# A one-core hybrid block (RWKV-7, Mamba-2, short convolution): opposite partition halves for head pairs, logits on two row halves, and the second scan moved behind the solve

## The reference, cut to what matters

```python
p = rmsnorm(x, norm_w) @ w_in
pa, pb, pc, pg = split(p)
def step(s, inp):                       # rwkv7, 16 heads of 64
    r_t, w_t, k_t, v_t, kh_t, b_t = inp
    sa = einsum('bhvk,bhk->bhv', s, kh_t)
    s = s * w_t[:, :, None, :] - sa[..., None] * b_t[:, :, None, :] + v_t[..., None] * k_t[:, :, None, :]
    return s, einsum('bhvk,bhk->bhv', s, r_t)
ob = mamba2_branch(pb)                  # conv of 4 taps, chunked scan (128), norm
oc = short_conv_branch(pc)
merged = sum(sigmoid(gates) * (o @ w_branch), axis=2)
out = rmsnorm(x + merged @ w_out, final_norm_w)
```

## Time and profile before

| what | us |
|---|---|
| median of 3 runs | 1234.29 (1234.07 to 1234.81) |
| the profiled execution: time, span | 1233.7, 1232.0 |
| PE busy | 1186.5 (96%) |
| VectorE busy | 798.4 (65%) |
| ScalarE busy | 578.0 (47%) |
| mean DMA rate | 160 GB/s |

### The profile page before, as it was taken

The page is one execution under the profiler, slowest core; times in us unless marked ns, Lnnn a source line. Parts: engine busy times, 40 slices in busy tenths (PEclk is TensorE's granted clock), DMA queues, the critical chain, the costliest instruction groups (busy, mean ns, idle before and its releaser), DMA issues.

```text
span 1232.0 us, 23862 instructions
## 1 busy us (share of the span) xinstructions
PE 1186.5 (96%) x8598; PEld 1057.4 (86%) x8598; DVE 798.4 (65%) x1229; ACT 578.0 (47%) x836; POOL 68.4 (6%) x93
## 2 busy tenths in 40 slices
PE   6998999999999999999999999999999999999996
PEld 5998899898898998989989978888888888888885
DVE  4786858678488585885876856564555565556553
ACT  5454445354364463544545535544444444434443
POOL 2001001010010010100101102000000000000000
PEclk9999999999999999999999999999999999999998
DMA  5755545544555354445554445566666666567662
GB/s 164 206 154 140 156 123 141 140 118 129 143 141 150 102 154 132 136 124 139 143 149 113 128 140 172 171 198 196 192 199 189 190 189 200 190 189 274 200 191 101
DMA packets 254749, 197.27 MB, mean 160 GB/s; under 512 B 23943, under 2 KB 207472, under 8 KB 254064
## 3 DMA queue, kind: packets, MB, share of 16 engines
q1 hardware_dynamic: 254404, 196.08, 55.1%
q10 hardware_dynamic: 300, 0.58, 0.1%
HBM read 193.71 MB, written 2.11 MB: 159 GB/s over the span
## 4 chain that ended last, share of the span: by engine, by line
PE 81%; DVE 11%; issue 3%; ACT 2%; DMA 1%; DVEq 1%; SPq 0%; POOL 0%; ACTq 0%
PE ps L1129 11%; PE ps L1207 11%; PE ps L1208 11%; PE ps L1209 11%; PE ps L1130 10%; PE ps L1131 10%; DVE lots L879 3%; DVE wlo L716 3%; PE ps L1460 2%; PE ps L1459 2%; PE ps L1461 2%; DVE lots L882 2%; ACT whi L421 1%; PE ps L1122 1%; DVE lots L724 1%
## 5 line engine op out<-in xcount | busy, mean ns | idle before, releaser
L716 DVE TENSOR_TENSOR wlo<-raw,whi 128x1024 fp32r<-128x1024 f32 (+1 forms) x356 | 436.0, 1238 | 278.7 <-ACT whi L421 278.1
L421 ACT ACTIVATE whi<-raw 128x1024 fp32r<-128x1024 f32 (+1 forms) x356 | 370.3, 1053 | 273.4 <-PE ps L1209 183.6
L1129 PE MATMUL ps<-hhi,whi 128*128 128x256 f32 (+1 forms) x1440 | 424.6, 295 | 5.7 <-DVE wlo L716 5.7
L1130 PE MATMUL ps<-hlo,whi 128*128 128x256 f32 (+1 forms) x1440 | 406.8, 282 | 0.0
L1131 PE MATMUL ps<-hhi,wlo 128*128 128x256 f32 (+1 forms) x1440 | 406.4, 282 | 0.0
L1129 PEld LDWEIGHTS ps<-hhi,whi 128*128 128x128 f32 (+1 forms) x1440 | 273.4, 190 | 22.6 <-issue 9.8
L1130 PEld LDWEIGHTS ps<-hlo,whi 128*128 128x128 f32 (+1 forms) x1440 | 274.0, 190 | 1.0
L1131 PEld LDWEIGHTS ps<-hhi,wlo 128*128 128x128 f32 (+1 forms) x1440 | 273.7, 190 | 0.3
L1207 PE MATMUL ps<-whi,hhi 128*128 128x512 f32 x384 | 151.4, 394 | 0.0
L1209 PE MATMUL ps<-whi,hlo 128*128 128x512 f32 x384 | 149.6, 390 | 0.0
L1208 PE MATMUL ps<-wlo,hhi 128*128 128x512 f32 x384 | 149.5, 389 | 0.0
(11 more groups left out here) (267 smaller groups left out, 1185.4 us busy)
## 6 DMA issues: line engine op xcount, KB each, us to landing
raw<-in_w_in SPq DMA_DIRECT2D x548, 256.0 KB, 3.2
raw<-in_w_branch SPq DMA_DIRECT2D x96, 256.0 KB, 3.7
raw<-in_w_out SPq DMA_DIRECT2D x64, 256.0 KB, 3.6
o<-in_x SPq DMA_DIRECT2D x4, 1024.0 KB, 6.9
acb<-acs_rows SPq DMA_DIRECT2D x8, 256.0 KB, 4.0
out_y<-lots SPq DMA_DIRECT2D x3, 512.0 KB, 4.6
lots<-in_final_norm_w SPq DMA_DIRECT2D x1, 1024.0 KB, 10.3
lots<-ad SPq DMA_DIRECT2D x32, 8.0 KB
```

Of the source, the lines that this page charges most:

```text
L421: sc.activation(whi[:, slot, :, 0:width], raw[:, slot, :, 0:width], ACT.Copy).then_inc(hi_done, 1)
L716: tt(wlo[:, slot, :, 0:width], raw[:, slot, :, 0:width], whi[:, slot, :, 0:width].bitcast(F32), ALU.subtract).then_inc(lo_done, 1)
L1129: mm(dst, a, khi, start=first, stop=False)
L1130: mm(dst, a, klo, start=False, stop=False)
```

## The change

- **Halves.** Head 0 keeps its state in partitions 0 to 63 and its identity in 64 to 127, head 1 the other way round. The products for `yz`, `nm` and the state then write opposite column halves for the two heads. The products with the identity (L1351) go; VectorE adds r times the decay to `yz` itself, in two instructions (`z_in`, slot 24). `gcs` and its products (L1331) go; each state row is scaled by VectorE straight from `gg`, in two instructions of 64 partitions instead of one.
- **Logits.** Each uses only its 64 rows, on its own row half, into two PSUM banks (A and C); PE waits for `var_rt` before it, and ScalarE takes the logits at slot 36 instead of 38.
- **Order.** Scores go one slot earlier (3, 5, 7). SyncE issues two `ad` transfers behind each quarter of a strip. The solve goes to slots 9 to 12; conv to 13, `seg` to 15, `xs2` to 18. The transposes of x go to slot 20 and `yb` to slot 22 on PE. Two of the four `tb` transfers are issued by ScalarE. The head norm goes to slot 34 around `kk_floor`, `kk_recip` and `decays` to 35.

```diff
+V_XT = 20
+V_YB = V_P1 + 4
...
-                strip(c + 8, cols, quarters=range(0, 2))
                 for q in range(4):
                     if q % 2 == 0:
+                        strip(c + 8, cols, quarters=range(q // 2, q // 2 + 1))
                         sp.wait_ge(s["ad_ok"], j * 2 + q // 2 + 1)
                     sp.dma_start(sol_n[8 * q:8 * q + 8, :, :], ad[:, q, :]).then_inc(s["n_in"], 16)
...
                 sp.wait_ge(s["sol_tr"], j + 1)
-                for q in range(4):
+                for q in range(2):
                     sp.dma_start(tb[:, q, :, :], sol_2[8 * q:8 * q + 8, :, :, :]).then_inc(s["t_in"], 16)
...
-                sc.activation(tanhs[:, 1, :], A[:, T:2 * T], ACT.Tanh, scale=0.5,
+                sc.activation(tanhs[:, 1, :], C[:, 0:T], ACT.Tanh, scale=0.5,
                               bias=halfb[:, bass.ds(j + CT, 1)]).then_inc(s["tanh_wa"], 1)
...
-                    if t == 5:
+                    if t == 4:
...
                     if t == 10:
-                        act.wait_ge(s["x_s"], j * 4 + 4)
-                        sc.activation(cvt, cv, ACT.Tanh, scale=0.5).then_inc(s["x_th"], 1)
...
+                    if t == 17:
+                        act.wait_ge(s["sol_tr"], j + 1)
+                        for q in range(2, 4):
+                            act.dma_start(tb[:, q, :, :], sol_2[8 * q:8 * q + 8, :, :, :]).then_inc(s["t_in"], 16)
+                        act.wait_ge(s["x_s"], j * 4 + 4)
+                        sc.activation(cvt, cv, ACT.Tanh, scale=0.5).then_inc(s["x_th"], 1)
...
                     if t == 36 and not last:
                         kk_root(j + 1)
-                    if t == 38 and not last:
                         half_logits(j + 1)
...
-            v.tensor_copy(st[0:64, :, :, :].rearrange("p e c n -> p (e c) n"),
-                          ident[0:64, 0:64].unsqueeze(1).broadcast_to([64, 2 * NC, 64]))
+            for e in range(2):
+                i = slice(64 - 64 * e, 128 - 64 * e)
+                v.tensor_copy(st[i, e, :, :], ident[i, i].unsqueeze(1).broadcast_to([64, NC, 64]))
...
-                    if t == 5:
+                    if t == 4:
                         scores(0)
-                    if t == 7:
+                    if t == 6:
                         scores(1)
...
+                    if t == V_P1 + 6:
+                        dve.wait_ge(s["yz_ok"], j + 1)
+                        for e in range(2):
+                            h = slice(64 * e, 64 * e + 64)
+                            op = tt(yz[h, e:4:2, :], yz[h, e:4:2, :], kr[h, :, 1, :], ALU.add)
+                        op.then_inc(s["z_in"], 1)
                     if t == V_P1 + 7:
                         for b in range(2):
                             dve.wait_ge(s["nm_mm"], j * 2 + b + 1)
-                            tt(nm[:, b].rearrange("p e c n -> p (e c) n"),
-                               ps[:, 6 + b, 0:2 * CPB * 64].rearrange("p (a n) -> p a n", n=64),
-                               ident[:, 64:128].unsqueeze(1).broadcast_to([P, 2 * CPB, 64]), ALU.add).then_inc(s["nm_ok"], 1)
+                            tt(nm[:, b], ps[:, 6 + b, 0:2 * CPB * 64].rearrange("p (e c n) -> p e c n", e=2, c=CPB),
+                               ident[:].rearrange("p (e n) -> p e n", e=2).unsqueeze(2).broadcast_to([P, 2, CPB, 64]),
+                               ALU.add).then_inc(s["nm_ok"], 1)
...
-                        dve.wait_ge(s["gc_ok"], j + 1)
                         dve.wait_ge(s["state_mm"], j * (NC - 1) + c + 1)
-                        tt(st[64:128, :, c + 1, :], A[64:128, 0:128].rearrange("p (e n) -> p e n", e=2),
-                           gcs[64:128, :, c:c + 1].broadcast_to([64, 2, 64]), ALU.mult).then_inc(s["state_ok"], 1)
+                        for e in range(2):
+                            h = slice(64 * e, 64 * e + 64)
+                            op = ts(st[h, e, c + 1, :], A[h, 0:64], gg[h, 0, CL * c + CL - 1:CL * c + CL], None, ALU.mult)
+                        op.then_inc(s["state_ok"], 1)
...
+                    if t == 8:
+                        stt(bon, sh[:, 0, :], col(RK), k2, ALU.mult, ALU.mult).then_inc(s["rk_ok"], 1)
                     if t == 9:
-                        dve.wait_ge(tile_out, nt + 1)
-                        conv4(s["x_s"], j * 4, j)
-                        stt(bon, sh[:, 0, :], col(RK), k2, ALU.mult, ALU.mult).then_inc(s["rk_ok"], 1)
+
+                        dve.wait_ge(s["n_in"], j * 64 + 64)
+                        for k in range(1, 5):
+                            solve_step(k)
                     if t == 10:
-
-                        dve.wait_ge(s["n_in"], j * 64 + 64)
-                        for k in range(1, 10):
+                        for k in range(5, 10):
                             solve_step(k)
-                            if k == 7:
-                                dve.wait_ge(s["x_th"], j + 1)
-                                stt(xs2, cvt, 1.0, cv, ALU.add, ALU.mult).then_inc(s["xs_ok"], 1)
                     if t == 11:
-                        for k in range(10, 13):
+                        for k in range(10, 12):
                             solve_step(k)
                     if t == 12:
-                        dve.wait_ge(s["dat_ok"], 1)
-                        dve.wait_ge(s["seg_e"], j + 1)
-                        for k in range(13, 16):
+                        for k in range(12, 16):
                             solve_step(k)
                         dve.wait_ge(s["sol_r"], j * 15 + 15)
                         v.tensor_copy(sol_l, sol_t.rearrange("p s t -> p t s")).then_inc(s["sol_tr"], 1)
+                    if t == 13:
+                        dve.wait_ge(tile_out, nt + 1)
+                        conv4(s["x_s"], j * 4, j)
+                    if t == 15:
+                        dve.wait_ge(s["dat_ok"], 1)
+                        dve.wait_ge(s["seg_e"], j + 1)
                         seg_times(0, 0)
                         seg_times(0, 1)
                         seg_times(1, 0)
                         seg_times(1, 1).then_inc(s["seg_g"], 1)
+                    if t == 18:
+                        dve.wait_ge(s["x_th"], j + 1)
+                        stt(xs2, cvt, 1.0, cv, ALU.add, ALU.mult).then_inc(s["xs_ok"], 1)
                     if t == V_P1 + 1:
                         dve.wait_ge(s["rk_mm"], j + 1)
                         tt(bon, E[:, T:2 * T], sh[:, 2, :], ALU.mult).then_inc(s["bon_ok"], 1)
...
-                    if t == 35 and not last:
-                        kk_floor(j + 1)
-                    if t == 36 and not last:
-                        kk_recip(j + 1)
-                    if t == 37 and not last:
-                        decays(j + 1)
-                    if t == V_ST + NC + 4:
+                    if t == 34:
                         dve.wait_ge(s["var_rt"], j + 1)
                         v.reciprocal(rin, nrm).then_inc(s["ln_v"], 1)
                         dve.wait_ge(s["ln_v"], j * 4 + 1)
                         tt(yo, yc, rin, ALU.mult).then_inc(s["ln_v"], 1)
+                    if t == 34 and not last:
+                        kk_floor(j + 1)
+                    if t == 34:
...
+                    if t == 35 and not last:
+                        kk_recip(j + 1)
+                        decays(j + 1)
...
                 pe.wait_ge(lora_in, j * 32 + 32)
-                mm(A[:, 0:T], lorat[:, 0, :], lr[:], start=True, stop=True)
-                mm(A[:, T:2 * T], lorat[:, 1, :], lr[:], start=True, stop=True).then_inc(s["lora_mm"], 1)
+                mm(A[:, 0:T], lorat[0:64, 0, :], lr[0:64, :], start=True, stop=True)
+                mm(C[:, 0:T], lorat[64:128, 1, :], lr[64:128, :], start=True, stop=True).then_inc(s["lora_mm"], 1)
...
                     if t == 34 and not last:
+                        pe.wait_ge(s["var_rt"], j + 1)
                         norm_and_logits(j + 1)
-                    if t == 4:
+                    if t == 3:
...
                     if t == V_P1 + 4:
                         pe.wait_ge(s["yx_ok"], j + 1)
-                        pe.wait_ge(s["bon_ok"], j + 1)
+                        pe.wait_ge(s["xst_ok"], j + 1)
+                        pe.wait_ge(s["seg_g"], j + 1)
                         for e in range(2):
-                            op = mm(E[64:128, T + NC * e:T + NC * e + NC], ident[:, 64 * e:64 * e + 64], gg[:, 0, CL - 1:T:CL],
-                                    start=True, stop=True)
-                        op.then_inc(s["gc_mm"], 1)
+                            h = slice(64 * e, 64 * e + 64)
+                            mm(C[h, 0:T], xst[:, 0, h], seg[:, e, 0:T], start=True, stop=False, skip_group_check=True)
+                            op = mm(C[h, P:T], xst[:, 1, h], seg[:, e, T:384], start=False, stop=True,
+                                    skip_group_check=True)
+                        op.then_inc(s["yb_mm"], 1)
...
                         for q in range(4):
```

(25 more changed lines are left out.)

26 lines of the change are left out of this document (9 added, 17 removed).

## The result

The changed kernel takes **1225.99 us** (median of 5 runs, 1225.34 to 1228.89) against 1234.29 before (5 runs, 1233.62 to 1234.81): ratio 0.994, 95% interval 0.9924 to 0.9956. The forecast was 1215, with 1207 to 1225 as its range. So the sign was right, and less than half of the gain came: 8.3 us instead of 19.0. The profiled execution took 1225.43 us for a span of 1223.7.

The account below looks back on a forecast made before the run. Each pass was taken as 26.40 us set by VectorE plus 54.60 set by PE. Per pass −0.52 − 2.00 + 0.15 for near ties = −2.37, over eight passes −19.0: 1215 us from 1234.3, range 1207 to 1225.

Parts of the forecast that it names:

- B: Stretch of a pass from `tx` to the next `adt`, 54.60 us, set by PE; its terms sum to −2.00.
- A: Stretch of a pass from `adt` to `tx`, 26.40 us, set by VectorE; forecast to fall by 0.52 to 25.88.
- Scores a slot earlier: PE's scores move from slot 4 to slot 3, one slot of strip matmuls less in B: −1.44 a pass.
- halves: Heads in opposite column halves, so eight records take the time of four: −0.44 at L1350 and −0.44 at L1366.
- state products: PE's slots 25 to 27: six records in the fuller half become four, −0.33 a pass.
- the logits: Two full products on PE become one pair on two row halves: −0.13 a pass.
- first chunk of the next pass: Near tie: VectorE's `kk_recip` and `decays` stand ahead of slot 36's split; taken as 0, upper end 0.6.
- The solve's input: Near tie: `ad` rows land at 291.1, VectorE ready at about 291.3; taken as 0, upper end 0.5.
- starved solve: Rival: last two `ad` transfers queue behind 512 KB of `raw`, VectorE waits before the solve; slower, 1246 if 4 us late; 0.06.
- The third state row: Near tie: two VectorE instructions instead of one, behind a split; taken as 0, upper end 0.3.
- the near ties all fall badly: Rival, together with halves that don't overlap: all three ties cost 1.4 instead of 0.15, giving 1225; chance 0.10.
- The markers: Proof of error: idle over 0.5 before the solve, `adt` to `tx` not 25.9, PE waiting between slot 18's block and scores.

Follow-up runs that it names:

- a3: Changed kernel with VectorE's `tx` moved to slot 15 and its `seg` products to slot 16 behind the split: 1212.84 us.
- h1: Kernel before with the halves alone; order, logits and the two `gcs` products on PE left as before: 1227.44 us.
- a2: Changed kernel with VectorE's third state row put ahead of its split of slot 28: 1224.42 us.
- f1: Changed kernel with the third state row ahead of the split (a2) and the `ad` and `raw` transfers of a6: 1215.41 us.
- a6: a4 with, besides, SyncE's second quarter of `raw` issued behind the `ad` transfers: 1218.94 us.
- a4: Changed kernel with the fourth `ad` transfer issued by ScalarE instead of SyncE: 1227.94 us.
- c5: a3 plus conv behind the split of slot 14, a2's state row, `t32` ahead of the split of slot 20 and a6's transfers: 1195.90 us.
- a1: Changed kernel with VectorE's first score group put ahead of its split of slot 4: 1245.99 us.

## Why the prediction was right and wrong

**Right: a pass is a stretch set by VectorE and one set by PE.** Taking 2.6 us of VectorE's work out from ahead of `tx` (a3) brought `tx` 2.46 sooner and gave 13.2 us in the run; taking work from PE behind `tx` gave what the rows said (h1: −1.18 of −1.21). PE's wait moved to slot 18, 2.4 us rather than the 3 to 4 forecast: the 1.44 of strips taken from B by the earlier scores are worked off in A. By the prediction's rows an estimate is 2.53 + 0.88 + 0.22 − 1.44 = 2.2 us, less what scores to `tx` shrinks (0.05 in this pass).

**Right: the terms of B.** Scores a slot earlier, `yb`, `gcs`, transposes, halves and state products together: 51.38 once the state row is out of the way (a2, f1), against 51.37. The one term that was off, the logits (−0.13; measured −0.02), is too small to show against the others.

**Right: A, without its tie.** Scores to `tx` 27.03 in a6 and f1, against 27.10. `z_in`, `kk_recip` and `decays` cost nothing, as said: the "first chunk of the next pass" was no loss.

**Wrong: "The solve's input", taken as 0.** The step that failed is to take the last packet for the landing: "the last small packets fell ... 1.6 after the last issue. With two, that is 288.75 + 0.71 + 1.6 = 291.1", and "the packets in the trace show no such receipt". The packets came where that says: 291.1 is 9.4 behind the scores of before, and in the changed kernel's passes from the second to the seventh the last 64-byte packets end 9.34 to 9.43 behind the scores (10.05 and 9.92 in the first and the last). VectorE was ready where the forecast had it, too (9.66, forecast 9.6). But the rows are released by the semaphore `n_in`, not by the packets. Its last DMA event in the trace comes 0.59 to 0.94 after the last packet in the changed kernel's eight passes, and the first solve step starts 0.02 to 0.03 behind it. The trace of before has such an event as well, 0.40 to 0.43 after the last packet, and nobody waited for it: VectorE came 1.8 us later. Measured: VectorE waits 0.42 to 1.01 us in each pass, 5.3 in the run, and scores to `tx` is 27.77 in the mean, 0.67 over the forecast: 5.4 us in eight passes.

The 512 KB of `raw` issued just ahead add to both parts. Without them (a6 against a4, in which the last issue ends at 7.5 and 7.7 behind the scores) the packets end at 8.67 instead of 9.4 and the event comes 0.4 later, at 9.05 to 9.09 in the passes from the second to the seventh, ahead of VectorE's 9.6. With the 0.4 of before alone the forecast's 9.4 would have become 9.8 and the wait 0.2; so the 0.2 to 0.5 more that the event takes behind bulk weigh as much or more. So the starved solve's mechanism, which I had called unlikely because "raw was issued as closely ahead" before, was at work on a small scale. It was issued as closely before, but then conv stood between, and VectorE came to the solve 12.94 behind the scores instead of 9.6: the cover was larger, not the landing earlier. The Trainium skill (DMA: Bandwidth & Descriptors, Anatomy of one DMA) puts most of a transfer's fixed cost of about 2.0 us behind its last byte; its figures are for transfers issued by GpSimd, these are SyncE's. By it I had written that a pass would cost 0.2 to 0.7 more; the trace agrees with that range, with 0.67, though the time behind the last packet is under 1 us here. I had not put it into the sum.

**Wrong: "The third state row", taken as 0, upper end 0.3.** Measured 0.40 a pass, 3.2 us in eight, in the changed kernel (a2 against it); h1 has the same wait of PE, 0.33 in the pass shown against 0.34. The row has two instructions where it had one, behind the split of slot 28; ahead of the split it costs nothing (a2: 51.38).

**Not in the sum: the clock.** Some 1.4 us for each pass in which it fell, one pass in the changed kernel's profiled execution, three in a2's. In the changed kernel it came behind the waits at slot 18 (0.90 and 1.47, with the strips of one slot between); the 2.5 us before, in four pieces over slots 16 to 18, never did in the profiled execution.

**Not in the sum: the first pass.** I let its scores come 1.44 earlier; they wait for VectorE's products there (PE stands 0.34 for them), and came 0.24 earlier (119.69 to 119.45): 1.2 us. This is read from one execution of each; in the other kernels they start from 118.8 to 119.9.

Together 5.4 + 3.2 + 1.4 + 1.2, less the 8 x 0.15 set aside for ties, are 10.0 of the 10.7 missing (1226.0 − 1215.3). The remaining 0.7 lies in the last pass and is not explained further. The rival "the near ties all fall badly" named 1225, and it is in the main what happened; I gave it, with the halves that don't overlap, 0.10. Two of its three ties fell beyond their ends (0.67 against 0.5, 0.40 against 0.3), the third cost nothing. The markers worked in part: idle time before the first solve step over 0.5 us, and a wait of PE between slot 18 and the scores, were both named as proof of an error, and both were there (the first in the mean, 0.66; in the pass shown it is 0.42). The stretch from `adt` to `tx`, also named, saw nothing.

## What to carry to other kernels

Take a step that was hidden by other work as exposed once that work moves away, and count its whole chain: the bulk transfer issued ahead of it in time, and the time from its last packet to its semaphore (0.4 us here, up to 1.0 behind bulk). Take a landing from the semaphore's event, not from the packets. Near ties taken at zero do not average out; here two of three fell badly in each of eight passes. Cut a loop at an event that both kernels reach by the same chain (here PE's scores), not at one that another engine's queue can shift. And where an engine sets a stretch, look what stands in its queue ahead of the one result that the other waits for: here `seg` and one split, worth 13 us (a3), more than all that the change itself brought. When a step is moved ahead of a split, follow the buffer that the split frees.

## What the runs showed of the hardware

- **A small transfer on another queue is still held up by bulk data.** ScalarE's `ad` transfer, its issue over 7.50 us behind the scores in both runs, had all its packets through by 9.3 with 512 KB issued on SyncE's queue just ahead of it (a4) and by 8.7 without (a6). The Trainium skill (DMA: Bandwidth & Descriptors, Issuing engines are not separate DMA queues) says that both queues run on the same engines and interleave; the trace agrees: the small packets came out among the last of the bulk.
- **The last packet is not yet the release.** From the end of the last 64-byte packet of `ad` to the last event of its semaphore it took 0.38 to 0.43 us where no bulk ended together with the rows (before, h1, a6, f1, c5), and 0.49 to 0.97 us where 512 KB ended together with them (all others). VectorE started 0.02 to 0.03 us after the event.
- **The clock falls after short waits, not only long ones.** Two waits of 0.90 and 1.47 us, 1.4 us of work between them, were followed by a stretch of 4 us with granted clock 0.61. In a1, with longer waits, it stood at 0.62 and 0.52 in two stretches of 4 us of the second pass, and fell in each of the other passes as well:

```profile
226.00:230.00 4.00, 1.52 (x13) 1.00 0.14 29
230.00:234.00 4.00, 2.96 (x14) 0.62 0.52 137
234.00:238.00 4.00, 4.00 (x48) 0.52 0.96 270
```

  It came in some passes of a kernel and not in others whose waits were alike; why is left open.
- **Two half-row products beside each other gain nothing here.** The logits as a pair take as long as one after the other over all rows (51.40 against 51.38 a stretch).
